# A 256-token two-block kernel: x^T laid out by the host, the first two weight blocks in float32 for both token tiles

## The reference, cut to what matters

```python
def rms_norm(x, g, eps=1e-6):
    y = xf * lax.rsqrt(jnp.mean(xf * xf, axis=-1, keepdims=True) + eps)
    return y * g
x = x + 0.5 * (silu(h @ wg) * (h @ wu)) @ wd        # h = rms_norm(x, ffn1_norm), wg and wu 1024 x 2816
...                                                 # a mixer, a second such layer, a gated MLP, an attention
```

## Time and profile before

| | us |
|---|---|
| median of 3 runs (lowest to highest) | 856.46 (856.23 to 857.0) |
| the profiled execution | 856.73 |
| its span, first to last instruction | 854.8 |
| TensorE busy | 845.8 (99%) |
| VectorE, ScalarE, GpSimd busy | 637.7, 529.2, 59.5 |

### The profile page before, as it was taken

One profiled execution on the slowest core, in us unless ns is written; L12 is line 12 of the kernel. 1 busy time (PEld: TensorE's weight loads), 2 busy tenths in 40 slices (PEclk: granted clock), 3 DMA queues, 4 the chain that ended last, 5 costly groups with the idle time before them and its releaser, 6 DMA issues.

```text
span 854.8 us, 11995 instructions
## 1 busy us (share of the span) xinstructions
PE 845.8 (99%) x4759; PEld 735.3 (86%) x4759; DVE 637.7 (75%) x808; ACT 529.2 (62%) x762; POOL 59.5 (7%) x65
## 2 busy tenths in 40 slices
PE   9999999999999999999999999999999999999997
PEld 8988888888889988888888887888888897888885
DVE  5999999987698656765466468758777677877873
ACT  6777777766575544653454356548666666676772
POOL 0022222210000000000000000100000001000001
PEclk9999999999999999999999999999999999999999
DMA  8976566655644655576446545576665654953501
GB/s 272 342 250 202 175 197 197 195 159 159 203 148 141 205 193 178 173 249 232 159 162 229 201 148 187 192 236 228 199 202 189 210 182 146 298 171 108 188 1 50
DMA packets 123847, 161.43 MB, mean 189 GB/s; under 512 B 3976, under 2 KB 111248, under 8 KB 123664
## 3 DMA queue, kind: packets, MB, share of 16 engines
q1 hardware_dynamic: 122176, 153.85, 54.8%
q0 software_dynamic: 1312, 6.29, 2.1%
q10 hardware_dynamic: 304, 0.53, 0.2%
HBM read 159.61 MB, written 1.05 MB: 188 GB/s over the span
## 4 chain that ended last, share of the span: by engine, by line
PE 97%; DVE 1%; ACT 1%; issue 1%; POOL 0%; POOLq 0%; DVEq 0%; ACTq 0%
PE pAcc L458 23%; PE pG L392 9%; PE pU L392 9%; PE pAcc L392 7%; PE pG L398 5%; PE pR L392 5%; PE pU L398 5%; PE pM L392 4%; PE pAcc L398 3%; PE pR L398 2%; PE pAcc L436 2%; PE pAcc L438 2%; PE pM L398 2%; PE pAcc L437 2%; PE pG L536 1%; PE pG L378 1%
## 5 line engine op out<-in xcount | busy, mean ns | idle before, releaser
L326 DVE TENSOR_TENSOR lo<-raw,hi 128x2048 fp32r<-128x2048 f32 x131 | 298.5, 2288 | 54.1 <-ACT hi L321 54.1
L321 ACT ACTIVATE hi<-raw 128x2048 fp32r<-128x2048 f32 x140 | 265.8, 1908 | 12.8 <-PE pU L379 3.1
L392 PE MATMUL pG<-xT,hi 128*128 128x512 f32 x336 | 83.4, 390 | 0.0
L392 PE MATMUL pU<-xT,hi 128*128 128x512 f32 x320 | 80.0, 392 | 0.0
L458 PE MATMUL pAcc<-hi,h_hi 128*128 128x512 f32 x240 | 74.5, 392 | 0.0
L392 PEld LDWEIGHTS pG<-xT,hi 128*128 128x128 f32 x336 | 62.8, 188 | 13.6 <-issue 0.7
L458 PE MATMUL pAcc<-lo,h_hi 128*128 128x512 f32 x240 | 74.0, 389 | 0.0
L458 PE MATMUL pAcc<-hi,h_lo 128*128 128x512 f32 x240 | 73.9, 389 | 0.0
L1173 ACT ACTIVATE h_hi<-h 128x512 fp32r<-128x512 f32 x28 | 17.7, 633 | 80.6 <-PE pAcc L458 74.8
L392 PEld LDWEIGHTS pU<-xT,hi 128*128 128x128 f32 x320 | 58.0, 189 | 10.7
L1709 DVE TENSOR_TENSOR h_lo<-h,h_hi 128x512 fp32r<-128x512 f32 x28 | 19.3, 688 | 45.9 <-ACT h_hi L1173 45.9
(11 more groups left out here) (522 smaller groups left out, 1637.0 us busy)
## 6 DMA issues: line engine op xcount, KB each, us to landing
raw<-in_a_w_in SPq DMA_DIRECT2D x24, 1024.0 KB, 5.2
raw<-in_ffn_wd SPq DMA_DIRECT2D x22, 1024.0 KB, 5.8
raw<-in_ffn_wg SPq DMA_DIRECT2D x21, 1024.0 KB, 5.4
raw<-in_ffn_wu SPq DMA_DIRECT2D x21, 1024.0 KB, 6.4
raw<-in_w_in SPq DMA_DIRECT2D x16, 1024.0 KB, 5.5
raw<-in_a_w_out SPq DMA_DIRECT2D x8, 1024.0 KB, 4.9
raw<-in_w_kv SPq DMA_DIRECT2D x8, 1024.0 KB, 5.4
raw<-in_b_w_qz SPq DMA_DIRECT2D x8, 1024.0 KB, 5.3
```

Of the source, the lines that this page charges most:

```text
L321: act.activation(HI[n % NHL][:, :], RAW[n % NRAW][:, :], ACT.Copy).then_inc(S["hi"], 1)
L326: dve.tensor_tensor(LO[n % NHL][:, :], RAW[n % NRAW][:, :], HI[n % NHL][:, :].bitcast(f32), ALU.subtract).then_inc(S["lo"], 1)
L392: end = pe.matmul(v3(bank[:, :], 2), wh[:, k, w], x4[:, :, k, :], start=start and k == 0, stop=not start and k == KD - 1, skip_group_check ...
```

## The change

- The host lays out x^T in the order of the four parts (input x_t); they are loaded to XRAW (the place of XN) on the queues where x went. TensorE's sixteen transposes of x fall away. x itself, for the residual, is loaded in one DMA of 1 MB later, ahead of block 8 (load_x); the first turn of the residual waits for it.
- The mean of squares is taken from x^T: ScalarE squares (square_first, with the output written so that the 8 chunks of a token lie side by side), VectorE sums over the 8 (sum_first), TensorE multiplies by a column of 1/1024 (mean_square), VectorE adds epsilon (variance_first).
- The first gain is loaded on GpSimd's queue behind the identity instead of ScalarE's.
- Block 1 is multiplied in float32 for tile 1 too; h of tile 1 is multiplied by its power later. Block 1 gets no hi and lo parts. Block 2's are made in halves (hi_first, lo_first).
- Block 4 is loaded when block 0 is used, block 5 when block 1 is used.
- Positions and tables come laid out by the host in two plain loads behind block 3, instead of four broadcasts ahead of it.

```diff
         def load_block(sp, n):
...
-            if n >= NRAW:
-                sp.wait_ge(S["lo"], n - NRAW + 1)
-            if n in (NRAW, NRAW + 1):
-                sp.wait_ge(S["used"], 1)
+            if n in (NRAW, NRAW + 1):
+                sp.wait_ge(S["used"], n - NRAW + 1)
+            elif n > NRAW:
+                sp.wait_ge(S["lo"], n - NRAW + 1)
...
+        def load_x_t(engine, b):
+            c = slice(b * 512, (b + 1) * 512)
+            engine.dma_start(XRAW[:, c], T["x_t"][:, c]).then_inc(S[f"x_in{b}"], 16)
...
+        def load_x(sp):
+            sp.wait_ge(S["x_sum"], 2)
+            sp.dma_start(v3(X[:, :], NT), T["x"][0].rearrange("(t p) c -> p t c", p=P)).then_inc(S["x_rows"], 16)
...
+        def mean_square(pe, t):
+            pe.wait_ge(S["x_sum"], t + 1)
+            pe.matmul(VAR[t], SSQ[:, t * P:(t + 1) * P], MEAN, start=True, stop=True).then_inc(S["x_var"], 1)
...
         def pe_start(pe):
-            busy(pe, 7)
-            x_transposes(pe, 0, 0)
-            pe.wait_ge(S["gain0"], 16)
+            busy(pe, 6)
+            pe.wait_ge(S["gain_first"], 16)
             pe.transpose(ACC[1][:, 0:KD], G8, IDENT[0:KD, 0:KD]).then_inc(S["gc_ps"], 1)
-            x_transposes(pe, 0, 1)
+            busy(pe, 3)
             pe.wait_ge(S["xf0"], 1)
             pe.wait_ge(S["first0"], 16)
             first_block(pe, 0, G, 0, range(0, 4))
             pe.wait_ge(S["xf1"], 1)
             pe.wait_ge(full[0], LANDED[0])
-            first_block(pe, 0, G, 0, range(4, 6))
+            first_block(pe, 0, G, 0, range(4, KD))
+            mean_square(pe, 0)
+            pe.wait_ge(S["xf2"], 1)
+            first_block(pe, 0, G, 1, range(0, 4))
             power_row(pe, 0)
-            first_block(pe, 0, G, 0, range(6, KD))
-            x_transposes(pe, 1, 0)
-            x_transposes(pe, 1, 1)
+            pe.wait_ge(S["xf3"], 1)
+            first_block(pe, 0, G, 1, range(4, 6))
+            mean_square(pe, 1)
+            first_block(pe, 0, G, 1, range(6, KD)).then_inc(S["used"], 1)
             pe.wait_ge(S["first1"], 16)
-            first_block(pe, 1, U, 0, range(0, 4))
+            first_block(pe, 1, U, 0, range(0, 2))
             power_row(pe, 1)
+            first_block(pe, 1, U, 0, range(2, 4))
             pe.wait_ge(full[1], LANDED[1])
             first_block(pe, 1, U, 0, range(4, KD))
-            pe.wait_ge(S["xf2"], 1)
-            pe.wait_ge(S["xf3"], 1)
-            first_block(pe, 0, G, 1, range(0, KD)).then_inc(S["used"], 1)
-            pe.wait_ge(S["lo"], 2)
-            pe.wait_ge(S["xt_lo"], 3)
-            to_tokens(pe, 1, U, XT, (1,), half_way=4).then_inc(S["used"], 1)
+            first_block(pe, 1, U, 1, range(0, KD)).then_inc(S["used"], 1)
+            pe.wait_ge(S["xt_lo"], 4)
...
         @block.sync
-            load_x(sp, 0, 0)
+            load_x_t(sp, 0)
             load_half(sp, 0, 0)
             load_half(sp, 0, 1)
-            load_x(sp, 1, 0)
-            load_x(sp, 1, 1)
+            load_x_t(sp, 2)
+            load_x_t(sp, 3)
             load_half(sp, 1, 0)
             load_half(sp, 1, 1)
             load_block(sp, 2)
-            ...                          # four small loads of positions and tables
             load_block(sp, 3)
+            sp.dma_start(POS[:, 0:TOK + NT], T["bias_positions"]).then_inc(S["bias_pos"], 16)
+            sp.dma_start(TABLES[:, 4 * NSTEP:], T["bias_tables"]).then_inc(S["bias_pos"], 16)
...
         @block.gpsimd
             pool.memset(IDENT[:, :], 0.0).then_inc(S["ident"], 1)
             pool.memset(HALF[:, :], -0.5).then_inc(S["half"], 1)
+            pool.memset(MEAN, 1.0 / D).then_inc(S["mean"], 1)
             pool.wait_ge(S["ident"], 1)
             pool.affine_select(out=IDENT[:, :], in_=IDENT[:, :], compare_op=ALU.not_equal, fill=1.0, base=0,
                                pattern=[[-1, P]], channel_multiplier=1).then_inc(S["ident"], 1)
+            load_gain_first(pool)
...
         @block.scalar
-            load_x(act, 0, 1)
-            load_gain_first(act)
+            load_x_t(act, 1)
             act.wait_ge(S["half"], 1)
             warm(act, ACT.Square)
-            for t in range(NT):
-                for c in range(2):
-                    act.wait_ge(S[f"x_in{t}{c}"], 16)
-                    square(act, 0, t, c)
+            for b in range(4):
+                square_first(act, b)
+            warm(act, ACT.Silu)
             xt_hi_first(act, 0)
             xt_hi_first(act, 1)
-            hi_half(act, 0)
-            hi_half(act, 1)
-            warm(act, ACT.Silu)
             xt_hi_first(act, 2)
             xt_hi_first(act, 3)
-            hi(act, 2)
+            hi_first(act, 0)
+            hi_first(act, 1)
...
         @block.vector
             xt_first(dve, 0)
             xt_first(dve, 1)
-            variance(dve, 0, 0)
+            sum_first(dve, 0)
+            xt_first(dve, 2)
+            xt_first(dve, 3)
+            variance_first(dve, 0)
+            sum_first(dve, 1)
             norm_first(dve, 0)
             norm_first(dve, 1)
-            variance(dve, 0, 1)
-            xt_first(dve, 2)
-            xt_first(dve, 3)
+            variance_first(dve, 1)
             xt_lo_first(dve, 0)
             xt_lo_first(dve, 1)
             norm_first(dve, 2)
             norm_first(dve, 3)
-            lo_of_half(dve, 0)
-            lo_of_half(dve, 1)
             xt_lo_first(dve, 2)
             xt_lo_first(dve, 3)
-            lo(dve, 2)
+            lo_first(dve, 0)
+            lo_first(dve, 1)
```

More of the change, by code:

```diff
@@ L57 @@
 NRAW, NHL = 4, 4
+UNSPLIT = 2
 LEAD = 3
@@ L100 @@
     "hi": "hi parts of weight blocks", "lo": "lo parts of weight blocks", "used": "weight blocks multiplied",
-    "x_in00": "x of token tile 0 loaded, its first half", "x_in01": "its second half",
-    "x_in10": "x of token tile 1 loaded, its first half", "x_in11": "its second half",
+    "x_in0": "x^T of token tile 0 loaded, its first half", "x_in1": "its second half",
+    "x_in2": "x^T of token tile 1 loaded, its first half", "x_in3": "its second half",
+    "x_sum": "squares of a token tile summed over the chunks of features",
+    "x_var": "and over the features of a chunk", "x_rows": "x loaded", "mean": "1 / D",
     "first0": "first half of weight block 0 loaded", "first1": "first half of weight block 1 loaded",
@@ L105 @@
     "xf2": "that of token tile 1, first half", "xf3": "its second half",
-    "gc_ps": "first gain by features in a bank", "gc": "and in SBUF", "rb": "powers of the first norm along columns",
-    "hi_first": "hi part of the first half of block 1",
+    "gain_first": "first gain loaded", "hi_first": "hi part of the first half of block 2", "gc_ps": "first gain by features in a bank", "gc": "and in SBUF", "rb": "powers of the first norm along columns",
     "const_in": "lambda vectors, subln gain and DFT matrices loaded",
@@ L296, in load_half, with hi_first, lo_first @@
                 full[n] if half else S[f"first{n}"], 16)
-        def hi_half(act, half):
-            act.wait_ge(*((full[1], LANDED[1]) if half else (S["first1"], 16)))
+        def hi_first(act, half):
+            if not half:
+                act.wait_ge(full[UNSPLIT], LANDED[UNSPLIT])
             c = slice(half * KD * BC // 2, (half + 1) * KD * BC // 2)
-            op = act.activation(HI[1][:, c], RAW[1][:, c], ACT.Copy)
-            if half:
[L305 to L314, removed]
+            op = act.activation(HI[UNSPLIT][:, c], RAW[UNSPLIT][:, c], ACT.Copy)
+            op.then_inc(*((S["hi"], UNSPLIT + 1) if half else (S["hi_first"], 1)))
+        def lo_first(dve, half):
+            dve.wait_ge(*((S["hi"], UNSPLIT + 1) if half else (S["hi_first"], 1)))
+            c = slice(half * KD * BC // 2, (half + 1) * KD * BC // 2)
+            op = dve.tensor_tensor(LO[UNSPLIT][:, c], RAW[UNSPLIT][:, c], HI[UNSPLIT][:, c].bitcast(f32), ALU.subtract)
+            if half:
+                op.then_inc(S["lo"], UNSPLIT + 1)
         def hi(act, n):
@@ L538, in first_block @@
             return end
[L540 to L546, removed]
         def power_row(pe, t):
@@ L1070, in rows @@
             dve.wait_ge(S["rsqrt"], RS_ORDER.index(what) + 1)
-            dve.wait_ge(S[f"gain{g % 2}"], 16 * (g // 2 + 1))
+            dve.wait_ge(S[f"gain{g % 2}"], 16 * (g // 2 + g % 2))
             for n in range(2):
@@ L1135, in xf, with x_raw, squares, square_first @@
             return v3(XTF[:, b * 512:(b + 1) * 512], 4)
+        def x_raw(b):
+            return v3(XRAW[:, b * 512:(b + 1) * 512], 4)
         def xt_first(dve, b):
-            dve.wait_ge(S["xt_ps"], b + 1)
-            dve.tensor_tensor(xf(b), v3(XBANK[b][:, :], 4), fbc(GC[:, 4 * (b % 2):4 * (b % 2) + 4], P),
+            dve.wait_ge(S[f"x_in{b}"], 16)
+            dve.tensor_tensor(xf(b), x_raw(b), fbc(GC[:, 4 * (b % 2):4 * (b % 2) + 4], P),
                               ALU.mult).then_inc(S[f"xf{b}"], 1)
+        def squares(t):
```

(20 more changed lines are left out.)

45 lines of the change are left out of this document (22 added, 23 removed).

## The result

The changed kernel takes 860.19 us (median of 6 runs, 859.56 to 861.34) against 856.97 for the one before (856.23 to 857.29): ratio 1.0043, 95% interval 1.0033 to 1.0053. It is slower by 0.4%. The forecast was 855.6, and its range ended at 860.0. Rival B gave 859.7, from +3.2 us; the profiled spans (first to last instruction) differ by 858.1 - 854.8 = 3.3.

What follows compares the result with a forecast made beforehand. TensorE's unbroken row of matmuls bounds the kernel, so only the opening counts: start -1.05, transposes -0.87, block 1 +0.56, mean squares +0.25, pace +0.15 give -0.96 from 856.46, 855.5, said as 855.6 us; range 855.1 to 860.0.

Steps and rivals of the forecast that it cites:

- Rival B: Opening: gain lands behind both halves of block 0, 7.35; start about 8.75, slow clock, +3.2 us, 859.7; chance 0.30.
- What bounds the kernel: TensorE, busy 845.8 of 854.8 us, has no hole behind the opening; time saved before gate 1 comes off the end.
- the unknown: when the gain lands: Opening: gain on GpSimd's queue, issued near 1.55, forecast to land unhindered at 4.0, in time; chance 0.38.
- the x halves: Argument for a timely gain: ScalarE's half of x landed within 0.2 us of SP's, on another queue.
- The rest of the sum: Opening up to gate 1, gain in time: start, transposes, block 1, mean squares and pace, together -0.96 us.
- The two mean-square matmuls: TensorE's opening: two one-column matmuls added, 0.12 us each, +0.25 us, bounds 0.1 and 0.8.
- the bound of 1.2: ScalarE's squares of 512 elements: some 0.6 us each; at twice that still summed at 8.0, in time for 9.4.
- step 3: Block 1, token tile 1: 24 fp32r instructions (2.88 us) become 16 float32 ones (3.44), +0.56 us.
- the thin cover: Before gate 1: block 2's lo part ready some 0.4 us early; once gone, each 0.1 us costs 0.1 us.
- Queues: SP's queue: block 3 lands near 17.6, block 4 goes near 13.5, block 5 near 20.3; these edits cost nothing.

Runs made afterwards that it cites:

- run 3: Changed kernel with the gain's DMA as GpSimd's first instruction, ahead of the identity; ratio 1.0012 to the kernel before.
- run 4: Changed kernel with SP holding back the second half of block 0 and all behind it until the gain has landed; ratio 1.0023 to the kernel before.
- run 2: Kernel before with one edit: its gain on GpSimd's queue behind the identity, with its own semaphore; ratio 1.0035 to the kernel before.
- run 1: Changed kernel with the gain back on ScalarE's queue, behind its part of x^T; ratio 0.9997 to the kernel before, span 855.1 us.
- run 5: Changed kernel with 19 dummy matmuls instead of 6, keeping TensorE busy until the gain lands; ratio 1.0025 to the kernel before.
- run 9: Changed kernel, gain on ScalarE's queue, squares held back until x^T's third part landed, their users on VectorE and TensorE moved later; ratio 1.0013 to the kernel before.
- run 6: Changed kernel, gain on ScalarE's queue, squares written side by side; ratio 0.9997 to the kernel before, span 854.5 us.
- run 7: Changed kernel, gain on ScalarE's queue, squares side by side, second variance between tile 0's two normed halves; ratio 0.9997 to the kernel before, span 854.4 us.
- run 10: Changed kernel, gain on ScalarE's queue, second variance between the normed halves, squares written to PSUM banks; ratio 1.0009 to the kernel before.
- run 8: Changed kernel, gain on ScalarE's queue, tile 0's squares held back until x^T's third part landed; ran once, 858.51 us against 856.75 before.

## Why the prediction was wrong

*What bounds the kernel.* This was right. Outside the opening nothing moved: the start of gate 1 moved by 3.24 us, the span by 3.3.

*The failed step* is "the unknown: when the gain lands", with its "unhindered ... landing at 4.0, in time. That is the forecast." It landed at 7.50. The earlier trace rows had shown a transfer of GpSimd's queue behind the load of SP's, and I let the x halves outweigh them. Those were on SP's and ScalarE's queues and said nothing about GpSimd's. The runs show that its landing follows what SP has issued ahead of it: 7.50 with both halves of block 0 ahead (changed kernel), 5.96 with the second half issued 0.4 us behind it (run 3), 5.9 with the second half held back (run 4). The first packet moves at 5.69, 4.79 and 4.84. It does not wait for the last byte of the second half (8.15 in the changed kernel, 7.55 in run 2, where the gain landed at 7.7), so how the engines share between the queues is not settled. The queue counts too: issued at 1.18 on ScalarE's queue, behind the same x^T and beside the same weights, the gain's packets were through by 3.9 (run 1). The estimate of 2 us plus the bytes' time that the Trainium skill gives ("DMA: Bandwidth & Descriptors", section "Anatomy of one DMA — SWDGE (gpsimd) path") is far off for such a busy moment: 5.8 us here, 4.2 at the least.

*Rival B* was right in the main and nearly in size: start at 8.75 (8.81), delay and lost clock +3.2 (+3.3). Its parts, from the runs: with the clock kept (run 5) the span is 2.0 above before, B had +1.77; the clock is 1.3, B had 1.5. Part of the match is luck. B let the gain land with the second half at 7.35; the second half came only at 8.15, and the gain's packets moved ahead of its end. B's return of the clock at 11.75 fits the 11.66 of the changed kernel, but in run 2 it came only at 13.63, with TensorE at work from 7.70. The Trainium skill's rule that an idle TensorE falls to 1.2 GHz ("TensorE: Matmul & The Clock Gate", section "Part 1: The HAM clock gate (the "warmup" mystery)") agrees with the granted clock of 0.56 and 0.59 behind 3.15 us without work. I gave B 0.30, the forecast 0.38; the weights were the mistake. The range was missed by 0.2 us, and that is no error of B's: the kernel before took 856.97 beside the changed one and not the 856.46 from which all sums start, and the difference of 3.2 is B's own.

*The rest of the sum* was -0.96 with the gain in time. Run 1 is that case. Its start was right to the hundredth (5.87), with some luck: the first half had landed at 5.66, and what TensorE finished last were its dummies, which began 0.2 us later than in the sum. But gate 1 came 0.3 later than before instead of 1 earlier. Mis-sized were the transfers, for which I had taken the rows of before: the second half came 0.6 later and the third part of x^T 1.8 later, which costs 0.3 to 0.5 us before the ninth instruction and 0.5 before the seventeenth. The second power row waited 0.27, since VectorE did two products ahead of the variance and GpSimd's power took 1.05 us, not 0.55. Together that is 1.1 to 1.3 us, about the distance from -0.96 to run 1's +0.28. The two mean-square matmuls cost 0.14 each (0.12 assumed). The squares took 1.04 us each, within the bound of 1.2. The sums took the row's 1.21. The last float32 tile of before ends at 18.30 and not at 18.47 (the first ordinary instruction behind it is spaced by 0.30 us and not by 0.12), so step 3 costs nearer 0.4 than 0.56, a small error. The lo part of block 2 was ready at 21.26 in run 1, 0.4 us ahead of gate 1: the thin cover was as forecast, and run 9 shows its price when it is gone.

*Queues.* Nothing was lost to the extra load of x or to the new conditions on blocks 4 and 5: TensorE has no further wait than before behind gate 1. The times given for the queue were off all the same. Taking the positions away did not free SP: the issue of block 3 now blocked it, and that of the positions again for 3.26 us:

```profile
5.52 4.51 SPq L294 DMA_DIRECT2D raw<-in_ffn_wu  x1
```

Block 3 landed at 19.0 instead of 17.6 (19.6 in run 1), and block 4 was issued at 17.96 instead of 13.5 (14.67 in run 1, without the late gain).

No version found here is clearly faster than the kernel before. Runs 1, 6 and 7 are 0.03% below it, inside their intervals.

## What to carry to other kernels

A small transfer on which a start hangs should not be moved to GpSimd's queue beside large ones: its size did not protect it, and the same 4 KB on ScalarE's queue were there 3 us earlier. If it must go there, its issue should come before the large ones' (run 3 got back 1.5 us of the landing by 0.4 us of issue time). When TensorE is made to wait near the start, the price is the wait and the slow clock behind it: here 2.0 and 1.3 us, and dummy matmuls through the wait give the second back. Most durations read from the trace of before held for the same instructions (GpSimd's power did not), but landings at full DMA load did not carry over to a new order, and where a sum of a microsecond rests on them it is not known to better than that microsecond.

## What the runs showed of the hardware that I had not expected

- A DMA on GpSimd's queue with 4 KB took 4.2, 4.7, 5.6, 5.8 and 6.0 us to land (runs 4, 3, 5, changed kernel, run 2), the more the more SP had issued ahead of it; most of it passes before the first packet moves (3.1 us in run 4, 4.0 in the changed kernel).
- ScalarE writing 512 floats 32 bytes apart into SBUF takes 1.04 us instead of about 0.6 (run 6, side by side), and 0.60 into a PSUM bank 16 bytes apart (run 10); VectorE summing over 8 values 512 bytes apart takes 1.91 us for 1024 elements instead of 1.21 side by side. What one engine gained by the layout the other lost in part.
- GpSimd's power of one column took 1.05 or 1.06 us where VectorE made lo parts of x^T beside it (L1182, two tensors of SBUF read; second place of the changed kernel and of runs 1, 3, 4, 5, 6 and 8), and 0.55 to 0.57 where VectorE summed, multiplied with a PSUM bank or stood idle (first place everywhere; second place of runs 7, 9 and 10).
- The second half of block 0, 512 KB, landed 5.5 (run 8) to 6.9 us (run 3) after its issue in the new opening, against 5.7 and 5.9 in the old (before, run 2); in run 4, where it was issued at about 6 when all ahead of it had landed, after 4.1.
- Issues on SP's queue took 0.4 to 0.9 us each in the first 5 us of the changed kernel, but the ninth of them, block 3, took 4.51 us and the positions behind it 3.26.
